# Stick-breaking attention: the last unit's minus absolute value made by VectorE in two operations

## What is computed

```
z = einsum('bhqd,bhkd->bhqk', q_b, kf) * scale
strict = s_pos[None, :] < tq[:, None]
log_beta = log_sigmoid(z)
log_1m = where(strict, log_beta - z, 0.0)
excl = cumsum(log_1m, axis=3, reverse=True) - log_1m
a = where(strict, exp(log_beta + excl), 0.0)
return einsum('bhqk,bhkd->bhqd', a, vf)
```

## Time and profile before

| | |
|---|---|
| Time, median of 3 runs (lowest to highest) | 1598.48 us (1597.65 to 1600.09) |
| Time of the profiled execution | 1599.97 us |
| Its span, first to last instruction | 1598.3 us |
| Mean granted clock of TensorE in it | 0.996 |
| PE busy | 1561.1 us, 98% of the span |
| DVE busy | 1172.8 us, 73% |
| ACT busy | 825.0 us, 52% |
| POOL busy | 84.9 us, 5% |
| DMA | 297.45 MB, mean 186 GB/s |

### The profile page before, as it was taken

The page is one execution under the profiler, slowest core; times in us unless marked ns, Lnnn a source line. Parts: engine busy times, 40 slices in busy tenths (PEclk is TensorE's granted clock), DMA queues, the critical chain, the costliest instruction groups (busy, mean ns, idle before and its releaser), DMA issues. The chain is left out here.

```text
span 1598.3 us, 36010 instructions
## 1 busy us (share of the span) xinstructions
PE 1561.1 (98%) x12314; PEld 1458.5 (91%) x12314; DVE 1172.8 (73%) x1793; ACT 825.0 (52%) x1351; POOL 84.9 (5%) x91
## 2 busy tenths in 40 slices
PE   8999999999999999999999999999999999999998
PEld 7978789999997879999989888899999999999997
DVE  5874788888877579998866556678888478676644
ACT  5564766553556576664455223235555355555533
POOL 2100001110300001110010100000000000000000
PEclk9999999999999999999999999999999999999999
DMA  9521444558742345558845643467888545455551
GB/s 364 189 84 44 155 154 167 174 191 274 264 148 78 110 154 171 176 178 291 313 133 195 202 143 133 144 223 281 280 270 280 191 159 185 156 197 183 179 182 47
DMA packets 84234, 297.45 MB, mean 186 GB/s; under 512 B 9664, under 2 KB 12480, under 8 KB 83392
## 3 DMA queue, kind: packets, MB, share of 16 engines
q1 hardware_dynamic: 78912, 283.24, 52.6%
q10 hardware_dynamic: 5248, 13.18, 2.4%
HBM read 291.40 MB, written 1.05 MB: 183 GB/s over the span
## 5 line engine op out<-in xcount | busy, mean ns | idle before, releaser
L1013 DVE TENSOR_TENSOR WL<-ring,WH 128x1024 fp32r<-128x1024 f32 x427 | 525.9, 1233 | 247.2 <-ACT WH L483 245.8
L483 ACT ACTIVATE WH<-ring 128x1024 fp32r (+1 forms) x419 | 441.6, 1057 | 510.9 <-PE projs L1711 242.1
L1711 PE MATMUL projs<-AH,WH 128*128 128x256 f32 (+2 forms) x2072 | 524.5, 290 | 11.4 <-ACT WH L483 3.8
L1711 PE MATMUL projs<-AL,WH 128*128 128x256 f32 (+2 forms) x2072 | 519.4, 287 | 0.3
L1711 PEld LDWEIGHTS projs<-AH,WH 128*128 128x128 f32 x2072 | 389.8, 189 | 24.6 <-DVE mk L1382 10.0
L1711 PEld LDWEIGHTS projs<-AL,WH 128*128 128x128 f32 x2072 | 392.4, 190 | 5.4 <-DVE AL L1173 1.7
L1711 PE MATMUL projs<-AH,WL 128*128 128x256 f32 (+2 forms) x2128 | 305.6, 285 | 0.2 <-DVE WL L1013 0.2
L1711 PEld LDWEIGHTS projs<-AH,WL 128*128 128x128 f32 x2128 | 276.7, 189 | 6.5 <-DVE WL L1013 2.5
L1711 PE MATMUL accs<-FH,WH 128*128 (+1 forms) x768 | 190.5, 284 | 2.0 <-ACT WH L483 2.0
L1711 PE MATMUL accs<-FL,WH 128*128 (+1 forms) x768 | 189.7, 281 | 0.0
L1711 PEld LDWEIGHTS accs<-FH,WH 128*128 128x128 f32 x768 | 144.3, 188 | 3.3 <-issue 3.3
(11 more groups left out here) (282 smaller groups left out, 1954.5 us busy)
## 6 DMA issues: line engine op xcount, KB each, us to landing
ring<-in_stream SPq DMA_DIRECT2D x532, 512.0 KB, 3.9
W1v<-in_w ACTq DMA_DIRECT2D x2, 1024.0 KB, 7.4
W1k<-in_w ACTq DMA_DIRECT2D x2, 1024.0 KB, 10.6
D<-in_decay ACTq DMA_DIRECT2D x4, 512.0 KB, 5.6
x<-in_xT SPq DMA_DIRECT2D x2, 512.0 KB, 4.9
memT<-in_memT SPq DMA_DIRECT2D x1, 1024.0 KB, 10.9
mq<-P ACTq DMA_DIRECT2D x8, 128.0 KB, 5.3
ctxT<-in_ctxT ACTq DMA_DIRECT2D x1, 1024.0 KB, 7.2
```

The costliest lines, as they stand in the source:

```text
L483: A(WH[:, s, :], ring[:, r % RING, :], ACT.Copy).then_inc(wh_ready, 1)
L1013: V.tensor_tensor(WL[:, s, :], ring[:, r % RING, :], WH[:, s, :].bitcast(F32), ALU.subtract).then_inc(consumed, 1)
L1711: return T.matmul(out, lhsT, rhs, start=start, stop=stop, skip_group_check=True)
```

## The change

In the last unit only (v = U - 1, which is unit 11 in each of the two layers), the Abs on ACT is replaced by two operations on DVE: max(z, 0) * -2 from PSUM into `prob`, then that plus z, which is -|z|. ACT takes the Exp of it without its scale of -1, then the Ln as before. The DVE operations stand in first(11); DVE waits there for turn(9), which frees the half of `scr`. In the attention to the memory no unit is a stick unit, and nothing changes.

```
@@ scalar engine
+                        if v == U - 1:
+                            n["low"] += 2
+                            act.wait_ge(low_ready, n["low"])
+                            chain.link(A(prob[:, :, 0:384], prob[:, :, 0:384], ACT.Exp))
+                        else:
+                            act.wait_ge(sc_ready, u + 1)
                             act.wait_ge(t_mm, u - 1)
-                        chain.link(A(prob[:, :, 0:384], score[:, :, 0:384], ACT.Abs))
-                        chain.link(A(prob[:, :, 0:384], prob[:, :, 0:384], ACT.Exp, scale=-1.0))
+                            chain.link(A(prob[:, :, 0:384], score[:, :, 0:384], ACT.Abs))
+                            chain.link(A(prob[:, :, 0:384], prob[:, :, 0:384], ACT.Exp, scale=-1.0))
                         A(prob[:, :, 0:384], prob[:, :, 0:384], ACT.Ln, bias=1.0).then_inc(ln_ready, 1)
@@ vector engine, first(v)
                     dve.wait_ge(sc_ready, u + 1)
                     if un["kind"] == "stick":
+                        if v == U - 1:
+                            dve.wait_ge(t_mm, u - 1)
+                            low = prob_of(u)[:, :, 0:384]
+                            V.tensor_scalar(low, scores_of(u)[:, :, 0:384], 0.0, -2.0, ALU.max, ALU.mult).then_inc(low_ready, 1)
+                            dve.wait_ge(low_ready, n["low"] + 1)
+                            V.tensor_tensor(low, low, scores_of(u)[:, :, 0:384], ALU.add).then_inc(low_ready, 1)
+                            n["low"] += 2
                         return
```

More of the change, by code:

```diff
@@ L364, in transformer @@
         bank_done = sem("bank_done")
+        low_ready = sem("low_ready")
         vm_ready = sem("vm_ready")
@@ L478, in _ @@
             chain = Chain(act, a_chain)
-            n = dict(norm=0, split=0, scaled=0, raw=0, x=0, q=0, u=0, soft=0, stick=0, o=0, tap=0, pair=0, conv=0, ret=0)
+            n = dict(norm=0, split=0, scaled=0, raw=0, x=0, q=0, u=0, low=0, soft=0, stick=0, o=0, tap=0, pair=0, conv=0, ret=0)
             def split(r, s):
@@ L640, in exps @@
                     if un["kind"] == "stick":
-                        act.wait_ge(sc_ready, u + 1)
-                        if u >= 2:
+                        if v == U - 1:
[4 more added lines that the diff above has]
+                            act.wait_ge(sc_ready, u + 1)
                             act.wait_ge(t_mm, u - 1)
-                        chain.link(A(prob[:, :, 0:384], score[:, :, 0:384], ACT.Abs))
-                        chain.link(A(prob[:, :, 0:384], prob[:, :, 0:384], ACT.Exp, scale=-1.0))
+                            chain.link(A(prob[:, :, 0:384], score[:, :, 0:384], ACT.Abs))
+                            chain.link(A(prob[:, :, 0:384], prob[:, :, 0:384], ACT.Exp, scale=-1.0))
                         A(prob[:, :, 0:384], prob[:, :, 0:384], ACT.Ln, bias=1.0).then_inc(ln_ready, 1)
@@ L1008, in _ @@
             chain = Chain(dve, v_chain)
-            n = dict(norm=0, split=0, q=0, u=0, soft=0, stick=0, o=0, tap=0, pair=0, silu=0, conv=0, gated=0, x=0, bank=0)
+            n = dict(norm=0, split=0, q=0, u=0, low=0, soft=0, stick=0, o=0, tap=0, pair=0, silu=0, conv=0, gated=0, x=0, bank=0)
             def split(r, p, s):
```

## The result

| | before | after |
|---|---|---|
| First comparison, median of 8 runs each | 1598.63 us (1597.65 to 1600.09) | 1603.07 us (1600.34 to 1604.42) |
| Ratio after to before | | 1.0023, 95% interval 1.0014 to 1.0032 |
| Second comparison, medians of 33 and 11 runs | 1599.09 us (1597.39 to 1600.67) | 1601.52 us (1598.47 to 1604.23) |
| Ratio | | 1.0013, 95% interval 1.0004 to 1.0022 |
| Profiled execution | 1599.97 us, span 1598.3 us | 1601.47 us, span 1599.8 us |

The change makes the kernel slower by some 0.1% to 0.3%; both intervals lie above 1. The ratio isn't that of the two medians, which would be 1.0028 and 1.0015: the runs lie in groups, four of the first eight at 1604.3 to 1604.4 us and four from 1600.3 to 1601.8 us, and the first median falls between them.

The account below looks back on a forecast made before the run. PE, 98% busy, was taken as the bound. Two delays of 0.98 us gave 1600.44 us from the median, 1601.93 us from the profiled run; the middle, 1601.2 us, was forecast, range 1598.8 to 1604.0 us.

Parts of the forecast that it names:

- Where it matters and what ends the pause: PE before turn(10), each layer: 2.18 us pause, ended by unit 10's chain of ACT, DVE's second(10) and POOL's cut.
- nothing behind takes the delay back: PE behind the attention, 545 to 1590 us: busy 1035.47 of 1045 us, so both delays count in full, 1.96 us.
- The delay on DVE, 0.98 us: DVE, each layer: two operations and out_block(7) ahead of second(10) start it 0.98 us later; PE's pause grows to 3.16 us.
- Both durations: DVE's two new operations in first(11): 0.96 us each, taken from the softplus row of the same size.
- the choice between the bounds: Duration of a new DVE operation: 0.96 us taken, between a low of 0.18 us (first only) and a high of 1.233 us.
- The VectorE rule of the Trainium skill: DVE reading PSUM: no two-port mode, an estimated 925 ns per operation, so a delay of 0.91 us per layer.
- The gain is nothing: ACT's unit 11: Ln ends 0.8 us earlier, worth nothing because turn(10) and values(9) on PE hide it.
- The clock: PE behind the attention's pause: the longer pause lowers the granted clock more often, up to one more stretch in the median run.
- the middle of the bounds: Median after: 1601.2 us, between 1600.44 us (clock unchanged) and 1601.93 us (both low stretches paid).
- The slower rival: turn(10) to values(10): clock falls in both layers in nearly every execution; 1601.93 or 1603.6 us; chance 0.40.
- The price of a stretch, 1.7 us: PE soon after the pause, each layer: 3.4 us at half clock cost 1.7 us.
- the median run pays for one and not for two: Kernel before: 1.49 us from profile (1599.97) to median (1598.48) is nearly one stretch, so the median pays one low stretch.

Follow-up runs that it names:

- the filled kernels: Zero matmuls in PE's pause: kernel before, 1597.81 us; change with out_block(7) ahead of its DVE operations, 1597.97; kernel before with ACT's unit 11 operations ahead of turned_copy(9), 1595.89.
- the wait alone: Kernel before with only DVE's wait for turn(9) added in first(11), without the two operations, ACT keeping its Abs: 1599.22 us, a single run.
- out_block(7) ahead: Changed kernel with out_block(7) put ahead of DVE's two operations, pause not filled: 1598.36 us, ratio 1.0006 to the kernel before.
- operations behind second(10): Changed kernel with DVE's two operations right after second(10) and ahead of out_block(8): 1599.92 us, ratio 1.0005 to the kernel before.
- Abs left out: Kernel before without ACT's Abs of the last unit and nothing in its place on DVE, result differs: 1599.80 us, ratio 1.0004.
- the last trace: Changed kernel, unaltered, traced once more in search of the runs near 1604.4 us: 1603.33 us.
- the half-filled kernel: Changed kernel, order kept, with 25 small zero matmuls in the second half of PE's pause: 1598.77 us, ratio 1.0001 to the kernel before.

## Why the prediction was right or wrong

The measure of a layer by what the clock did behind the pause, from all the traces, the filled kernels among them (the row "before" takes in the wait alone):

| us per layer | high | low once (3.4 us) | low for 6.8 us |
|---|---|---|---|
| before (pause 2.18 us) | 9.44 | 10.57 to 10.61 | not seen |
| change (pause 3.22 us) | 10.05 | 11.4 to 11.7 | 12.96 |
| out_block(7) ahead (pause 2.81 us) | 9.64 | 11.29 | not seen |
| operations behind second(10) (pause 2.18 us) | 10.61 | 10.62 | not seen |
| Abs left out (pause 2.18 us) | 9.01 | 10.53 | not seen |

- **Where it matters and what ends the pause**: right. The wait for POOL's cut grew in both layers. That nothing behind takes the delay back was right but for some 0.4 us at the norm near 800 us, whose cause is open.
- **The delay on DVE, 0.98 us**: right, measured 1.04 us (3.22 - 2.18). Both durations were right (0.96, 0.95 us) and so was the choice between the bounds. The missing 0.06 us and a little more are the start behind turn(9): 133.56 against a modelled end of 133.45, so 0.11 us instead of 0.03.
- **The VectorE rule of the Trainium skill** (VectorE: DVE Perf Modes, the table of "The TRN2 errata" and "Why PSUM operands drop a tier") gave 0.925 us as an estimate for an operation with a PSUM source; 0.96 us were measured for the one-input form. That such an operation isn't twice as fast is what the skill says there, and the trace agrees.
- **"The gain is nothing"**: wrong as a general step, and this is the step that failed. It was read in a trace whose both layers were at the low clock, where turn(10) and values(9) are slow enough to cover unit 11's chain. At the high clock they don't: PE waits 0.37 us for unit 11, and the relief of ACT is worth 9.45 - 9.01 = 0.44 us per layer. So the change costs 10.05 - 9.44 = 0.61 us per layer there, and the full 1.04 (0.8 to 1.1 by the measure, 11.43 - 10.61 to 11.71 - 10.57) only at the low clock.
- **The clock**: right as a mechanism and undersized. The sum had it at 0.75 us over both layers, the middle of the bounds. The median rose by 4.44 and by 2.43 us in the two comparisons; the delay by itself accounts for 1.2 us (high clock) to 2.1 us (low), so roughly 0.3 to 3.2 us are left for the clock, the scatter at the start of the kernel among them. In the traces the clock fell behind 4 of 8 pauses of 2.18 us and behind 7 of 8 of 3.22 us, once for 6.8 us. As an estimate from these few: the mean measure is 10.02 us in the four layers of the order before and 11.56 us in the eight of the change, so 3.1 us for both layers together, 1.2 of them the delay. With the delay in place but the pause half filled the kernel is at 1598.77 us. The slower rival had described this, at turn(10) to values(10), with one stretch of low clock more, or two. It had the stretches one by one; that two can follow on each other behind one pause was shown in one trace.
- **The price of a stretch, 1.7 us, and "the median run pays for one and not for two"**: not borne out. In the order before a stretch behind the pause cost 1.1 to 1.2 us (10.57 and 10.61 against 9.44), since the wait for unit 11 goes with it; in the changed kernel 1.4 to 1.7 us. And the 1.49 us from profile to median were laid to the attention alone, while the profiled execution had a third stretch, at 11.5 to 14.9 us, which the prediction doesn't have. The trace of the wait alone shows a run of 1599.22 us with no stretch in the attention and 6.8 us at the start.
- **How the steady part and the clock share the loss in a median** stays open within the bounds above, because the runs of both kernels scatter by 3 to 6 us with the clock.
- **The range and the chances**: the range held; 0.40 for slower was the case that came in the first comparison (1.0023), the second (1.0013) is on the other side of the line at 0.2%. The forecast's value was the middle between two bounds of one mechanism; with the failed step mended it would have been lower by up to 0.9 us, and so further off. The two errors had opposite signs, so that the number came as near as it did is in part luck.

## What to carry to other kernels

Before moving work to an engine that is less busy, look at what stands behind the place in its queue: here 1.9 us of DVE work for a unit that had time to spare stood ahead of the one operation for which PE stood still. A pause of PE has a second price, the clock behind it, and that price may be larger than the pause's growth; comparing with the pause filled by cheap matmuls tells the two apart. Look at the clock over the whole span first: a low stretch elsewhere, here at the start, can pass for the one under study. And a slack that was read behind a stretch of low clock is the slack of that execution: ask what is late next when PE runs at full speed.

## What the runs showed of the hardware

- Behind eight pauses of PE of 3.22 us, all in one kernel, the clock stayed at 1.00 once, was at 0.50 for 3.4 us six times and for 6.8 us once (layer 1 of the last trace). Behind eight pauses of 2.18 us it stayed four times and was at 0.50 for 3.4 us four times; behind two of 2.81 us one time each. After the pauses of 1.65 us that remained in the half-filled kernel it stayed at 1.00.
- The same 12 matmuls took 2.02 us at 1.00 and 3.79 us at 0.50 (layer 1 of the last trace). With small matmuls of zeros in the pause (128 columns, 0.06 us each: 34 in 2.07 us) the clock stayed at 1.00 in all eight layers that were traced.
- The clock near the start of the kernel varies as well (at 0.50 for 0, 3.4 or 6.8 us), in versions that don't differ there. Between two traces of one kernel, 3.4 us more of it cost 1.33 us.
- A DVE operation that waits for matmuls starts 0.1 us after their modelled end (0.11 us: 133.45 to 133.56); one that waits for DVE itself 0.03 us (133.56 + 0.96 to 134.55).
